# Attention taken in units of one query tile, with the next unit's scores issued ahead, and 64-row scores written in pairs of 512 keys

## The reference, cut to what matters

```python
# block 1, "a": 8 heads of 64, three dilated causal windows mixed by their log-sum-exp
y_a = dilated_mixture(qa, ka, va)
# block 1, "b": 8 heads of 64, one shared key/value head, only the 256 keys that an indexer picks
s = jnp.einsum('bqhd,bqkd->bhqk', q_blk, k_sel) * ATTN_SCALE
p = jax.nn.softmax(jnp.where(valid[:, None], s, -jnp.inf), axis=-1)
# block 2, "d": 4 heads, two maps of 64 each, bias by distance, all 1024 keys
s = jnp.einsum('bqhmd,bkhmd->bmhqk', qblk, k) * scale + bias
p = jax.nn.softmax(s, axis=-1)
a = p[:, 0] - lam * p[:, 1]
# block 2, "m": 4 heads, 128 + 64 channels per score, all 1024 keys
s = jnp.einsum('bqhd,bkhd->bhqk', qblk, k) * scale
```

## Time and profile before

| | |
|---|---|
| runs | 3541.32, 3541.97 and 3542.25 us; median 3541.97 us |
| span of the profiled execution, first to last instruction | 3530.3 us |
| median of the runs less that span | 11.7 us |
| PE busy | 3256.4 us (92%) |
| DVE busy | 1357.0 us (38%) |
| attention "a" with its fillers | 236.8 to 640.0 us |
| attention "b" with its fillers | 723.6 to 961.0 us |
| attention "d" with its fillers | 1940.0 to 2331.2 us |
| attention "m" with its fillers | 2430.1 to 2712.7 us |

### The profile page before, as it was taken

The page is one execution under the profiler, slowest core; times in us unless marked ns, Lnnn a source line. Parts: engine busy times, 40 slices in busy tenths (PEclk is TensorE's granted clock), DMA queues, the critical chain, the costliest instruction groups (busy, mean ns, idle before and its releaser), DMA issues. The chain is left out here.

```text
span 3530.3 us, 36411 instructions
## 1 busy us (share of the span) xinstructions
PE 3256.4 (92%) x14286; PEld 2424.8 (69%) x14286; DVE 1357.0 (38%) x2077; ACT 947.8 (27%) x1344; POOL 992.3 (28%) x416
## 2 busy tenths in 40 slices
PE   5998988988899999999998998886999999999998
PEld 3556666766578788888876565463445788888887
DVE  4358888688632111111124444534333221212122
ACT  3233233223632211111123333432333211111110
POOL 4322331431034342342454000012000342424241
PEclk8988999989999999999999899898999999999999
DMA  6311111220051111111113001010001111111112
GB/s 161 90 36 42 54 48 30 61 59 31 1 190 49 48 48 48 48 48 54 43 42 110 13 29 32 4 33 24 6 0 60 48 48 48 52 43 54 42 53 66
DMA packets 261611, 176.20 MB, mean 50 GB/s; under 512 B 20660, under 2 KB 248884, under 8 KB 260916
## 3 DMA queue, kind: packets, MB, share of 16 engines
q1 hardware_dynamic: 261496, 174.64, 17.0%
HBM read 142.60 MB, written 25.20 MB: 48 GB/s over the span
## 5 line engine op out<-in xcount | busy, mean ns | idle before, releaser
L676 PE MATMUL big<-g_hi,w_hi 128*128 128x512 f32 x3328 | 1051.9, 398 | 33.1 <-POOL w_lo L1641 19.0
L676 PE MATMUL big<-g_lo,w_hi 128*128 128x512 f32 x3328 | 1038.0, 393 | 0.0
L676 PE MATMUL big<-g_hi,w_lo 128*128 128x512 f32 x3328 | 1035.8, 393 | 0.0
L676 PEld LDWEIGHTS big<-g_hi,w_hi 128*128 128x128 f32 x3328 | 631.8, 191 | 183.3 <-issue 32.7
L676 PEld LDWEIGHTS big<-g_lo,w_hi 128*128 128x128 f32 x3328 | 634.0, 190 | 135.6
L676 PEld LDWEIGHTS big<-g_hi,w_lo 128*128 128x128 f32 x3328 | 631.6, 190 | 134.5
L1641 POOL TENSOR_TENSOR w_lo<-w_raw,w_hi 128x1024 fp32r<-128x1024 f32 x99 | 242.4, 2448 | 1066.5 <-ACT w_hi L974 1066.5
L1719 POOL TENSOR_TENSOR w_lo<-w_raw,w_hi 128x1024 fp32r<-128x1024 f32 x76 | 181.9, 2393 | 64.2 <-ACT w_hi L1177 64.2
L1584 DVE TENSOR_TENSOR x_res<-big,x_res 128x1024 f32 x40 | 49.0, 1225 | 382.1 <-PE big L676 382.1
L1442 DVE MAX8 m<-idx_acc 128x8 f32<-128x384 f32 (+5 forms) x192 | 171.6, 894 | 21.7 <-POOL qb L1668 16.0
L1745 POOL TENSOR_TENSOR w_lo<-w_raw,w_hi 128x1024 fp32r<-128x1024 f32 x40 | 95.7, 2392 | 273.2 <-ACT w_hi L1205 273.2
(11 more groups left out here) (238 smaller groups left out, 3359.2 us busy)
## 6 DMA issues: line engine op xcount, KB each, us to landing
w_raw<-in_w_up SPq DMA_DIRECT2D x54, 512.0 KB, 3.9
w_raw<-in_w_in SPq DMA_DIRECT2D x51, 512.0 KB, 4.2
w_raw<-in_w_down SPq DMA_DIRECT2D x48, 512.0 KB, 4.0
w_raw<-in_w_gate SPq DMA_DIRECT2D x22, 512.0 KB, 3.7
rot<-rope_in SPq DMA_DIRECT2D x68, 128.0 KB, 2.3
x_res<-x_spill SPq DMA_DIRECT2D x2, 4096.0 KB, 14.6
w_raw<-in_w_out SPq DMA_DIRECT2D x16, 512.0 KB, 4.1
g_spill<-gst_a SPq DMA_DIRECT2D x9, 512.0 KB, 3.0
```

Source lines behind the costliest of these rows:

```text
L676: ins = pe.matmul(out[0:m, HALF * h:HALF * h + HALF], w[slot][:, col:col + m], x[:, HALF * h:HALF * h + HALF], start=(n == 0 and q == 0), ...
```

## The change

`attend` and `attend_pairs` take the place of `pipeline`. The unit of `sc` and `nm` is now one query tile: for "a" and "b" a unit is a step, for "d" and "m" a step is two units, and `pv` still works on whole steps. The order of `S` becomes `nm(n)`, `pv(n-1)`, `sc(n+1)`, `topk`, filler of n for "a" and "b", and `sc(u+1)`, `nm(u)`, `pv` of the step before if u is the first of its step, filler of u for "d" and "m". "a" and "d" run through their four head groups as one list. In "d" and "m" the fillers are spread over the units of a head.

For "a", "b" and "d" a score job is no longer one map of up to 1024 keys in a `big` buffer; it is 512 keys of both lanes (or both maps), one in each bank of the buffer. Rows of over 512 keys come in two parts. The second part's minimum starts from that of the first (`mnp`), and DVE waits for the first part's end before it. "m" keeps one job of 1024 keys. DVE's wait before it writes `prob` again is for the transposes of the step two before, where it was for their products.

```diff
@@ -396,35 +396,50 @@
     a_steps = {c: [("a", c, i, 0) for i in range(QT)] for c in range(4)}
     b_steps = [("b", c, i, 0) for i in range(QT) for c in range(4)]
 
-    def pipeline(steps, filler={}, rest=0.0, before=None, carry=None):
-
-
-        prev = carry
-        for n, s in enumerate(steps):
-            if before:
-                before(s)
-            add("sc", s)
-            topk(rest * (s[2] + 1) / 2 + (FILL_TOPK if n in filler and filler[n][0][0] != "v_t" else 0.0) if rest else 0.0)
-            add("nm", s)
-            if prev:
-                add("pv", prev)
-            prev = s
+    def attend(units, filler, rest, before=None):
+
+        if before:
+            before(units[0])
+        add("sc", units[0], 0)
+        for n, s in enumerate(units):
+            add("nm", s, 0)
+            if n:
+                add("pv", units[n - 1])
+            if n + 1 < len(units):
+                if before:
+                    before(units[n + 1])
+                add("sc", units[n + 1], 0)
+            topk(rest * (s[2] + 1) / 2 + (FILL_TOPK if n in filler and filler[n][0][0] != "v_t" else 0.0))
             for f in filler.get(n, []):
                 add(*f)
-        return prev
+        return units[-1]
+
+    def attend_pairs(units, filler):
+
+        add("sc", *units[0])
+        for n, (s, ti) in enumerate(units):
+            if n + 1 < len(units):
+                add("sc", *units[n + 1])
+            add("nm", s, ti)
+            if ti == 0 and n:
+                add("pv", units[n - 1][0])
+            for f in filler.get(n, []):
+                add(*f)
+        return units[-1][0]
 
...
-    carry = None
     gate = iter(range(16))
+    filler = {}
     for c in range(4):
-        filler = {0: [("gate", next(gate))], 1: [("gate", next(gate))]}
+        filler[8 * c] = [("gate", next(gate))]
+        filler[8 * c + 1] = [("gate", next(gate))]
         if c < 3:
-            filler[2] = [("rope", f"qa{c + 1}")]
-            filler[3] = [("rope", f"ka{c + 1}")]
-            filler[5] = [("lin", f"va{c + 1}")]
-            filler[6] = [("v_t", f"va{c + 1}")]
-        carry = pipeline(a_steps[c], filler, A_TOPK, carry=carry)
+            filler[8 * c + 2] = [("rope", f"qa{c + 1}")]
...
     add("dv0")
     add("v_t", "dv0")
-    carry = None
+    filler = {}
     for h in range(4):
-        filler = {}
-        if h == 3:
-            filler[1] = [("donorm", h - 1)]
+        u = 8 * h
         if h < 3:
-            filler[0] = [("lin", f"dv{h + 1}"), ("lin", f"dq{h + 1}")]
-            filler[1] = [("v_t", f"dv{h + 1}")] + ([("donorm", h - 1)] if h else []) + [("lin", f"dk{h + 1}"), ("dnorm", "dq", h + 1)]
-            filler[2] = [("dnorm", "dk", h + 1)]
-        carry = pipeline(d_steps[h], filler, carry=carry)
+            filler[u + 1] = [("lin", f"dv{h + 1}")]
+            filler[u + 2] = [("v_t", f"dv{h + 1}")] + ([("donorm", h - 1)] if h else [])
+            filler[u + 3] = [("lin", f"dq{h + 1}")]
+            filler[u + 4] = [("dnorm", "dq", h + 1)]
+            filler[u + 5] = [("lin", f"dk{h + 1}")]
+            filler[u + 6] = [("dnorm", "dk", h + 1)]
+        else:
+            filler[u + 2] = [("donorm", h - 1)]
+    carry = attend_pairs([(s, ti) for h in range(4) for s in d_steps[h] for ti in range(2)], filler)
     add("pv", carry)
     add("donorm", 3)
...
@@ -497,18 +515,19 @@
     add("mn2", "k", 0)
     add("mh", 1)
     add("v_t", "mv1")
-    carry = None
+    filler = {}
     for h in range(4):
-        filler = {}
+        u = 8 * h
         if h == 3:
-            filler = {0: [("y2split", 4), ("y2split", 5)], 1: [("y2split", 6), ("y2split", 7)],
-                      2: [("y2split", 0), ("y2split", 1), ("y2split", 2)]}
-        if h < 3:
-            filler[0] = [("mn1", "q", h + 1), ("mn2", "q", h + 1)]
-            filler[1] = [("mn1", "k", h + 1), ("mn2", "k", h + 1)]
+            filler[u + 1] = [("y2split", 4), ("y2split", 5)]
+            filler[u + 3] = [("y2split", 6), ("y2split", 7)]
+            filler[u + 5] = [("y2split", 0), ("y2split", 1), ("y2split", 2)]
+        else:
+            filler[u + 1] = [("mn1", "q", h + 1), ("mn2", "q", h + 1)]
+            filler[u + 3] = [("mn1", "k", h + 1), ("mn2", "k", h + 1)]
             if h < 2:
-                filler[2] = [("mh", h + 2), ("v_t", f"mv{h + 2}")]
-        carry = pipeline(m_steps[h], filler, carry=carry)
+                filler[u + 5] = [("mh", h + 2), ("v_t", f"mv{h + 2}")]
+    carry = attend_pairs([(s, ti) for h in range(4) for s in m_steps[h] for ti in range(2)], filler)
     add("pv", carry)
     add("y2split", 3)
...
@@ -569,12 +588,33 @@
                     v=lambda kt, lane: mvb[c][:, kt, :], heads=False, prob=[mprob], pt=mpt if c else dpt, scale=MLA_SCALE, bias=None,
                     y=ym[:, c, cols_])
 
-    steps = [x[1] for x in S if x[0] == "sc"]
+    steps = list(dict.fromkeys(x[1] for x in S if x[0] == "sc"))
     Y2_ORDER = [x[1] for x in S if x[0] == "y2split"]
     nstep = {s: n for n, s in enumerate(steps)}
 
     def keys(st, i):
         return P * (i + 1) if st["causal"] else T
+
+    def lanes(st, ti):
+
+        if st["heads"]:
+            return [(lane, st["tiles"][lane], 0) for lane in range(2)]
+        return [(ti, st["tiles"][ti], m) for m in range(st["n_maps"])]
+
+    def parts_of_row(s, ti):
+
+        if s[0] == "m":
+            return [(0, T)]
+        st = step_of(s)
+        n1 = keys(st, st["tiles"][ti])
+        return [(n0, min(n0 + HALF, n1)) for n0 in range(0, n1, HALF)]
+
+    def score_key(s, ti, part=-1):
+
+        return ("sc", *s, ti, part % len(parts_of_row(s, ti)))
+
+    def final_score(s):
+        return score_key(s, 0 if s[0] in "ab" else 1)
 
     def tgroups(st):
...
@@ -810,17 +850,18 @@
                     "d": lambda: (s_hn.at("dq", c), s_hn.at("dk", c)),
                     "m": lambda: (s_hn.at("mq", c), s_hn.at("mk", c)),
                 }[kind]())
-                for ti, i in enumerate(st["tiles"]):
-                    for m, parts in enumerate(st["maps"](ti)):
-                        key = ("sc",) + s + (ti, m)
-                        out = take(key, s_rel)
-                        n1 = keys(st, i)
-                        for n0 in range(0, n1, HALF):
-                            ne = min(n0 + HALF, n1)
-                            for q, (qa, ka) in enumerate(parts):
-                                ins = pe.matmul(out[:, n0:ne], qa[:, P * i:P * i + P], ka[:, n0:ne], start=q == 0,
-                                                stop=q == len(parts) - 1)
-                        ins.then_inc(*s_big.mark(*key))
+                for part, (k0, k1) in enumerate(parts_of_row(s, ti)):
+                    key = score_key(s, ti, part)
+                    out = take(key, s_rel)
+                    for n0 in range(k0, k1, HALF):
+                        ne = min(n0 + HALF, k1)
+                        for at_, (lane, i, m) in enumerate(lanes(st, ti)):
+                            o = HALF * at_ + n0 - k0
+                            terms = st["maps"](lane)[m]
+                            for q, (qa, ka) in enumerate(terms):
+                                ins = pe.matmul(out[:, o:o + ne - n0], qa[:, P * i:P * i + P], ka[:, n0:ne], start=q == 0,
+                                                stop=q == len(terms) - 1)
+                    ins.then_inc(*s_big.mark(*key))
             elif stage == "pv":
                 s, = x
...
@@ -1450,44 +1489,46 @@
                     dve.tensor_scalar(z, z, -3.2e38, MASKED, ALU.is_gt, ALU.mult).then_inc(*s_tk.mark("mask", i))
                 dve.wait_ge(s_tk.sem, s_tk.count)
             elif stage == "sc":
-                s, = x
+                s, ti = x
+                st = step_of(s)
+                n = nstep[s]
+                if n >= 2:
+                    old = steps[n - 2]
+                    dve.wait_ge(*s_tb.at(old, len(tgroups(step_of(old))) - 1))
+                if s[0] == "a" and n == 0:
+                    dve.wait_ge(*s_cst[2].at())
+                if s == m_steps[0][0]:
+
+                    dve.wait_ge(*s_rot.at("uqr", 1))
+                if s[0] == "d":
+                    dve.wait_ge(*s_bl[s[1] % 2].at(s[1]))
+                spans = parts_of_row(s, ti)
+                for part, (k0, k1) in enumerate(spans):
+                    key = score_key(s, ti, part)
+                    dve.wait_ge(*s_big.at(*key))
+                    if part:
+                        dve.wait_ge(*s_rel.at(*score_key(s, ti, part - 1)))
+                    for at_, (lane, i, m) in enumerate(lanes(st, ti)):
+                        p = st["prob"][m][n % 2][:, lane, k0:k1]
+                        c = 4 * (n % 2) + 2 * lane + m
+                        ps = big[pair[key]][:, HALF * at_:HALF * at_ + k1 - k0]
+                        low = (mn if part == len(spans) - 1 else mnp)[:, c:c + 1]
+                        if st["bias"] is None:
```

(40 more changed lines are left out.)

## The result

The changed kernel takes 3561.3 us (median of 7 runs, 3550.9 to 3572.2) against 3542.3 us before (7 runs, 3532.8 to 3544.8): ratio 1.0054, 95% interval 1.0035 to 1.0072. It is 19 us slower, where 35 us less were forecast.

What follows compares the result with a forecast made beforehand. PE, busy for 92% of the span, was taken to bound the kernel. The terms −26 ("a") −5 ("b") −22 ("d") +18 ("m") = −35 us gave 3507 us, with an 8 in 10 range from 3462 to 3548 us.

Steps and rivals of the forecast that it cites:

- "a", −16 for the scaled row: In "a", 16.5 of 22.2 us of PE waits for the scaled row go, as scaling runs under the filler.
- +7: In "a", a filler's first job waits some 1.1 us for two evictions, six times: +7 us.
- rival 3: DVE is the bound in "a" and "b", so nothing is gained there: −4, 3538 us; chance 0.13.
- "a", −17 for the lanes: In "a", both lanes in one buffer no longer start staggered behind 17 fillers, 1.0 us each: −17 us.
- "b", −5: In "b", two gains of −17 together, limited by DVE to 11 us, taken as −5; bounds −11 and +3.
- two parts can only cost there: In "b" behind 855 us, where PE is dense without fillers, two-part rows only cost; upper bound of "b" +3 us.
- "d", −22: In "d", one-tile units: −41 from a warm layout, +19 for nine later norm sums; bounds −41 and +20.
- had already: In "d", the gain from two maps at once, −32 us if still open, is there already where buffers are free.
- "m", +18: In "m", six norms without `pv` ahead wait 29.0 instead of 13.8 us, +15, plus +3; bounds +9 and +25.
- The +3 for the clock: In "m", PE runs more of what follows the norm sums at half clock: +3 us.
- 1 and 4: 1: norms hide, PE keeps full clock, −78, 3464 us, chance 0.20; 4: evictions still pace "d", −13, 3529 us, 0.07.
- Rival 2: Half clock in every unit of "d", "d" +43, total +30, 3572 us; chance 0.13.

Runs made afterwards that it cites:

- e4: Changed kernel with two of POOL's three rotary operations for heads 1 to 3 of "a" on 64 of 1024 columns; 3542.4 us, ratio 1.0000.
- e1: Changed kernel with "a" and "b" in the old order of stages, score jobs still in parts; 3531.7 us, ratio 0.9976 to before.
- e9: Changed kernel with "a", "b" in old order, pairs there only up to 512 keys, norms of "m" behind `pv`; 3490.6 us, ratio 0.9845.
- e13: Changed kernel with all four attentions in the old order, pairs of 512 keys for all rows of "a", "b", "d"; 3483.1 us, ratio 0.9827.
- e14: e13 with lane 0's exponential in "a" and "b" released by the end of its own last part; 3464.2 us, ratio 0.9782.
- e8: Changed kernel with "d" in its old order and old fillers, pairs of 512 keys kept; 3530.3 us, ratio 0.9968.
- e6: Changed kernel with whole maps of 1024 keys as score jobs in "d", order of units kept; 3584.8 us, ratio 1.0121.
- e12: Changed kernel with each filler of "d" one unit earlier; 3595.6 us, ratio 1.0150.
- e10: Changed kernel with old orders everywhere, pairs for all rows in "d", up to 512 keys in "a" and "b"; 3461.7 us, ratio 0.9781.
- e2: Changed kernel with the norms of "m" one unit earlier, behind `pv` as before the change; 3531.9 us, ratio 0.9981.

## Why the prediction was wrong

Between −35 and +19 lie 54 us: 32 of them in "a", 17 in "b", 5 in "m" and none in "d".

- **"a", −16 for the scaled row:** right as a wait (22.2 to 6.5 us), wrong as a gain. The step "in the new order they run under about 11 us of filler" failed: on DVE the scalings stand ahead of the next scores' evictions, and on PE the filler stands behind those scores, so it waits for the scalings too. I had costed the filler's wait from two evictions with DVE free (+7); with POOL holding the scalings it was 24.6 + 1.7, half of it POOL's by e4. This is the case where the Trainium skill's exclusive lock of the shared port pair ("SBUF — State Buffer", section Who interferes with whom) spoke against the change; the scalings of 768 keys at 2.52 and 2.50 us beside POOL agree with it, where one of 640 keys took 0.55 us in the same kernel while POOL stood still. I used it only for DVE's total load, and rival 3 was the nearest to what happened, though in "a" DVE was no bound: it was busy for 353 of 410 us (86%) and late at the wrong moments. What stood behind the moved evictions had to be priced, not DVE's share.
- **"a", −17 for the lanes:** right, 14 us in e1 and 18 in e9, and in the changed kernel PE is busy for 341.3 us in "a" where it was for 359.5. In the order of the change it was used up by the waits for `va` (+8.4) and `pt` (+10.8), which I had not listed though the flush of the exponentials ahead of each filler was in the text.
- **"b", −5:** wrong, +12. Ahead of the first long step it is 2.8 us less (160.2 to 157.4 us), behind it 14.7 more (100.8 to 115.5). The gain ahead of it was to be up to 11: there PE was busy for 122.1 us instead of 135.1, but the wait for the scaled row went up to 23.1 us with DVE busy for 145.0 of 157.4 us (92%), so in this part rival 3 is what the rows look like. Behind it, "two parts can only cost there", bounded at +3, was undersized: I counted DVE's added time as lying beside PE and overlooked that ACT's order puts `pt` behind the exponential (e13, e14).
- **"d", −22:** the size came out to the microsecond, and so nearly did the four heads (88.9, 102.3, 102.3 and 72.5 us for 90, 101, 101 and 73), by luck: the account behind it was wrong. I had −41 from waits that go and +19 for norms that come late. The norm sums waited less instead, 5.0 us for 14.2; the units brought new waits of 17.9, 11.1 and 6.6 us (10.3 for 3.7), so that PE waits 17 us more in all; and the gain is in PE's own time, 38 us less busy. One row was taken for too many steps besides: 16.8 us is the first step of the last head, whose next two took 20.9 (with a norm behind it) and, at full clock, 14.3 us in the kernel before, so 3.7 us weren't there to gain in each of four. By the runs the pairs with the earlier exponentials are worth −50 (e8), the units +28 on top of them, and the units without the pairs −9.5 (e6). Where I wrote that two maps at a time were "had already", the row was right for tile 0 only.
- **"m", +18:** the mechanism right, the size a little short: +22 to +24 in the executions other than the profiled one. The sums have +16.5 of it, where I had +15. The rest of the waits wasn't in the sum: +2.6 for the copies of the transposes (6.7 for 4.1) and +1.4 for the scaled row, which PE did not wait for before. The +3 for the clock is near: PE is busy for 262.1 us in e12 and 263.9 in e1, for 258.7 in the earlier trace rows.
- **Rivals:** 1 and 4 didn't occur. Rival 2 (half clock in every unit of "d") neither: it went up to 0.94. The slower outcome came from a mechanism that I had only as a +7 term. The time lies beyond my range for the same reason: its upper end was set by the bounds of "m" and by a zero in "a" and "b", and I had no case in which these two lose.
- "m" takes 275.6 us in e10 and e13 and 282.6 before, with the same jobs and the same order but for ACT's exponentials. A step without a filler takes 14.26 us for 14.57, both at full clock, and the 0.31 us are in its last eight products with v, 1.98 us for 2.29: in the kernel before, an exponential stood in front of the last copy they need, and it now runs ahead of `pv`. The rest of the 7 us, in the steps with norms, isn't separated from the clock (0.98 for 0.97).

## What to carry over

Price a moved stage by what then stands behind it on every queue: a filler put between the scores and their use hides the wait of one engine only if the filler itself needs nothing that the scores hold. A buffer job that fills both halves of the array's rows and both banks at once was worth 14 to 18 us in "a", where the only reordering that gained, the units of "d" without pairs, was worth 9.5. Test the layout and the order apart before combining them, since the old order with pairs was 81 us faster than the kernel before (e10) and the new order cost 78 with them (e13 against the changed kernel). And when a stage is split in two, look for what else hangs on the stage's borders: here ACT's list of exponentials did. Where two executions are compared, see first whether each is typical of its runs.

## What the runs showed of the hardware

Pauses of PE cost more than their length: in "m" 16.4 us of waits before six sums (13.9 us in e2, 30.3 in the changed kernel's code) go with 24 to 26 us of time in seven executions, at a granted clock of 0.93 in e1 against 0.98 in e2. What the clock was before a stage counts as well: "m" with the same code took 304.4 to 306.4 us in seven executions and 316.7 in the one that came into it at half clock.

The page "TensorEngine Tiling (Array Packing)" of the Trainium skill, section Key Properties, says that different tiles run their matmuls in parallel. The runs agree: two maps of 64 rows take 1.99 us for 8 matmuls. How much of it is had hangs on when the buffers come free: with the second lane's buffer released by a copy of 1.02 us, 8 matmuls of 896 keys took 2.95 us.
